# Layer-norm sums with 128 output columns, idle products on TensorE, twelve partial means ahead of the last convolution, and a weight split behind the transposes

## The chip, the cores and the metric

The kernel runs on one core of a Trainium2 chip. The metric is the device time of one launch in microseconds. TensorE multiplies (and its clock has two levels here, 1.2 and 2.4 GHz), VectorE, ScalarE and GpSimd work element by element, SyncE issues DMAs. The engines run their own instruction streams and meet at semaphores.

## What is computed

One step of a streaming encoder with two layers, for 1024 prompt frames and 8 streams of 16 frames (1152 columns in all), model width 1024, float32. The change lies in the convolution module of layer 0 and in the last norm:

```python
def conv_module(h, buf, w_pw1, b_pw1, w_dw, b_dw, ln_g, ln_b, w_pw2, b_pw2):
    u = h @ w_pw1 + b_pw1
    a, gt = jnp.split(u, 2, axis=-1)
    glu = a * jax.nn.sigmoid(gt)
    xp = jnp.concatenate([buf.astype(glu.dtype), glu], axis=1)
    new_buf = xp[:, xp.shape[1] - (CONV_K - 1):]
    y = causal_dwconv(xp, w_dw, b_dw)          # 31 taps for each channel
    y = jax.nn.silu(layernorm(y, ln_g, ln_b))
    return y @ w_pw2 + b_pw2, new_buf

def rmsnorm(x, g):                             # also the last step of all
    y = x * lax.rsqrt(jnp.mean(x * x, axis=-1, keepdims=True) + EPS)
    return y * g
```

Behind it stand a ConvFFN, an HGRN2 mixer with its own ConvFFN, and the final RMSNorm.

## The kernel before

Activations lie by features: X holds 8 channel blocks (KD) of 128 partitions by 1152 columns, worked in three thirds of 384 (`third(c)`, NCH = 3). A float32 product is made of three products of high and low parts (XH, XL, WH, WL), 384 columns each, into one of two sets of three PSUM banks (`ps_bank(n, c)`; n is the number of the tile, its parity the set). MB are the two remaining banks. Weights come in 196 units of 128x1024, loaded by SP into two slots, split by GpSimd into high and low parts (`split(u)`: a cast and a subtraction), and used by TensorE in `big`.

First pointwise convolution: tiles G and V of each channel block go to VectorE, which forms the GLU. The depthwise convolution of blocks 0, 2 and 4 is done tap by tap on VectorE; that of the blocks 1, 3, 5, 6, 7 (TOEPLITZ) on TensorE: VectorE transposes the GLU in 32x32 pieces (`forward`, which raises `xt_rdy`), eight DMAs bring the taps as small Toeplitz matrices (`blocks`), TensorE makes 32 groups of two products with 40 columns (`convolved`), ScalarE copies the banks out (`by_blocks`) and VectorE transposes back (`back`). A float32 product of this kind leaves two MATMUL records in the profile; a high or low part leaves one. For blocks 1, 3, 5 and 6 the convolution is woven into the products of the next V tile. Block 7 has no such tile behind it. There TensorE weaves in the layer norm's mean: `mean(k, c)` multiplies channel block k of third c with a matrix of -1/1024, accumulated over k; 21 of these (blocks 0 to 6) are the list `parts`. Seven of them stand ahead of the convolution of block 7 and 14 between its two-group steps (16 steps); three for block 7 (L745, waiting for `back(7)`) stand behind it.

Then the layer norm, by thirds. `centred` (VectorE, L1763, 8 instructions a third) adds bias and mean, `ln_squares` (ScalarE) squares, GpSimd adds squares in pairs (L593), and `variance(c)` (L822) sums over channels: for each of four pairs and three pieces of 128 tokens, the squares are the stationary side and a column of ones the moving side, so that one output column holds 128 sums. ScalarE takes the root (`ln_root`), VectorE the reciprocal, spread on a diagonal (`diagonal`, L1770 and L1772), TensorE multiplies the diagonal with ones (`spread_norm`, L834), VectorE scales (`ln_scaled`, L1782), ScalarE applies gain, bias and SiLU (L1349) and casts every second block (L1352; GpSimd the others), VectorE forms the low part (`ln_low`, L1790), and TensorE begins the second pointwise convolution (`ln_row`, L857).

The order on each engine is the order of the program text: no planner, only waits on semaphores. GpSimd's splits of units U_PW2 and U_PW2 + 1 (the first two of the second pointwise convolution) follow the splits of the first one at once; behind them stand the pair sums and the casts of the norm. SP loads a unit when the split of the unit two before it is done.

The final norm has the same shape: `fin_sum` (L1164), the root, `fin_diagonal`, `fin_over` (L1179, spread), `scaled_out` on VectorE (L2205) and GpSimd's share, and the output DMAs.

Of the kernel before, what the change touches and what calls it, by code (L numbers as in the profile page):

```python
# [6 lines left out]
ACT = mybir.ActivationFunctionType  # L7
# [5 lines left out]
P = 128  # L13
D = 1024
# [3 lines left out]
KD = D // P  # L18
# [4 lines left out]
TOEPLITZ = (1, 3, 5, 6, 7)  # L23
BLK = 32
# [8 lines left out]
NCH = 3  # L33
COLS = SEQ // BLK + NB
BANK_GROUPS = 12
CW = T // NCH
# [27 lines left out]
T_PW2 = T_PW1 + len(PW1)  # L64
# [31 lines left out]
T_MEAN, T_VAR = pw1_tile("MEAN", 0), pw1_tile("VAR", 0)  # L96
# [78 lines left out]
def build(nc, d_w, d_x, d_par, d_taps, d_ffp, d_fhist, d_chist, d_state, d_const, d_mask,  # L175
          o_y, o_convp, o_convs, o_hgp, o_hgs, o_ffn):
    with ExitStack() as ctx:
# [15 lines left out]
        CONST = sb("CONST", [P, 2 * P + NB])  # L193
        IDENT = CONST[:, 0:P]
        ONES = CONST[:, P:2 * P]
# [3 lines left out]
        EPSC = SMALL[:, 0:1]  # L199
        LB = SMALL[:, 1:1 + KD]  # L200
        OMLB = SMALL[:, 1 + KD:1 + 2 * KD]
        R9 = SMALL[:, 1 + 2 * KD:1 + 2 * KD + TCH]
# [45 lines left out]
        LSQ = cut(NCH * KD, CW, of=HGA)  # L248
# [45 lines left out]
        PS, MB = BANKS[:, 0:2 * NCH, :], BANKS[:, 2 * NCH:8, :]  # L294
# [6 lines left out]
        def ps_bank(n, c):  # L301
            return PS[:, (n % 2) * NCH + c, 0:CW]
# [42 lines left out]
        xt_rdy, bt_rdy, bt_free, str_rdy = sem("xt_rdy"), sem("bt_rdy"), sem("bt_free"), sem("str_rdy")  # L345
# [175 lines left out]
        def _(pool):  # L521
            def split(u, i=0, per=0, used=None):


                s = u % 2
                pool.wait_ge(raw_ld[s], lin(i, 8 * per, raw_count(u)))
                if U_HG <= u - 2 < U_WO:
                    pool.wait_ge(a_full, u - 2 - U_HG + 1)
                elif used is None and u >= 2:
                    used = (unit_tile(u - 2) + 1, 0)  # L530
                if used is not None:
                    pool.wait_ge(ps_full, lin(i, used[1], used[0]))

                one = WRAW[:, s, 0:1]
                nc.gpsimd.tensor_tensor(PAD, one, one, ALU.mult)  # L535
                nc.gpsimd.tensor_copy(WH[:, s, :], WRAW[:, s, :]).then_inc(w_hi, 1)  # L536
                pool.wait_ge(w_hi, lin(i, per, u + 1))
                nc.gpsimd.tensor_tensor(WL[:, s, :], WRAW[:, s, :], WH[:, s, :].bitcast(F32),  # L538
                                        ALU.subtract).then_inc(w_split, 1)
# [44 lines left out]
            nc.gpsimd.memset(WT_FLAT[:, half:], 0.0).then_inc(wt_zero, 1)  # L584
            for u in range(3, U_PW2):
                split(u)
            split(U_PW2)
            split(U_PW2 + 1)

# [42 lines left out]
        def _(pe):  # L632
            def free_slot(n, i=0, per=0):

                if per or n >= 2:
                    pe.wait_ge(ps_free[n % 2], lin(i, per // 2, n // 2))
# [101 lines left out]
            def mean(k, c):  # L738

                if c == 0 and k in TOEPLITZ:  # L740
                    pe.wait_ge(bt_free, TOEPLITZ.index(k) + 1)
                    pe.wait_ge(str_rdy, TOEPLITZ.index(k) + 1)
                elif c == 0:
                    pe.wait_ge(taps_done, len([c for c in range(k + 1) if c not in TOEPLITZ]))
                ins = nc.tensor.matmul(ps_bank(T_MEAN, c), NEG_MEAN, X[:, k, third(c)], start=False, stop=k == KD - 1,  # L745
                                       skip_group_check=True)
                if k == KD - 1:
                    ins.then_inc(mean_full, 1)
# [43 lines left out]
            for c in range(1, KD):  # L792
                if c > 1:
                    big(pw1_tile("G", c), U_PW1 + 2 * c)
                big(pw1_tile("V", c), U_PW1 + 2 * c + 1, between=with_conv(c - 1) if c - 1 in TOEPLITZ else None)

            free_slot(T_MEAN)
            pe.wait_ge(mg_rdy, 1)
            for c in range(NCH):
# [1 line left out]
                                 skip_group_check=True)  # L801

            parts = [(k, c) for k in range(KD - 1) for c in range(NCH)]
            ahead = len(parts) - (BLK // 2 - 2)
            for k, c in parts[:ahead]:
                mean(k, c)
            for g in range(0, BLK, 2):
                convolved(KD - 1, g, g + 2)
                if g // 2 < len(parts) - ahead:
                    mean(*parts[ahead + g // 2])  # L810
            for c in range(NCH):
                mean(KD - 1, c)

            def variance(c):

                if c == 0:
                    free_slot(T_VAR)
                for p in range(KD // 2):
                    pe.wait_ge(pair_rdy, KD // 2 * c + p + 1)
                    for t in range(NCH):  # L820

                        ins = nc.tensor.matmul(ps_bank(T_VAR, c)[:, t:t + 1],  # L822
                                               LSQ[:, KD * c + 2 * p, t * P:(t + 1) * P], ONES[:, 0:1],
                                               start=p == 0 and t == 0, stop=p == KD // 2 - 1 and t == NCH - 1,
                                               skip_group_check=True)
                ins.then_inc(var_full, 1)

            def spread_norm(c):

                pe.wait_ge(yd_rdy, c + 1)  # L830
                if c == 2:
                    pe.wait_ge(yn_rdy, KD)
                for t in range(NCH):
                    ins = nc.tensor.matmul(MB[:, c % 2, t * P:(t + 1) * P], ONES,  # L834
                                           DIAG[:, c * CW + t * P:c * CW + (t + 1) * P], start=True, stop=True)
                ins.then_inc(spread_full, 1)

            variance(0)
            variance(1)
            spread_norm(0)  # L840
            variance(2)
            spread_norm(1)
            spread_norm(2)

            pe.wait_ge(w_split, U_PW2 + 2)
            free_slot(T_PW2)
            free_slot(T_PW2 + 1)

            def ln_row(j, c, k):
# [14 lines left out]
            for j in range(2):  # L866
                for k in range(KD):
                    ins = ln_row(j, NCH - 1, k)
# [284 lines left out]
            def fin_sum(c):  # L1153

                if c == 0:
                    pe.wait_ge(mb_free, M_FIN)
                pe.wait_ge(acc_rdy, c + 1)
                for squares in (ACC, SQ[:, 1, :]):
                    if squares is not ACC:
                        pe.wait_ge(last_sq, c + 1)  # L1160
                    for t in range(NCH):
                        a = c * CW + t * P

                        ins = nc.tensor.matmul(MB[:, c % 2, t:t + 1], squares[:, a:a + P], ONES[:, 0:1],  # L1164
                                               start=squares is ACC and t == 0,
                                               stop=squares is not ACC and t == NCH - 1, skip_group_check=True)
                ins.then_inc(fin_sums, 1)
# [27 lines left out]
        def _(act):  # L1195
# [135 lines left out]
            def ln_root(c):  # L1331

                act.wait_ge(var_full, c + 1)
                A(R9[:, c * NCH:(c + 1) * NCH], ps_bank(T_VAR, c)[:, 0:NCH], ACT.Sqrt, bias=EPSC, scale=1.0 / D
                  ).then_inc(root_rdy, 1)

            ln_squares(0)
# [212 lines left out]
                A(SQ[:, 1, third(c)], X[:, KD - 1, third(c)], ACT.Square).then_inc(last_sq, 1)  # L1550
            for c in range(NCH):
                act.wait_ge(fin_sums, c + 1)
                A(R9[:, c * NCH:(c + 1) * NCH], MB[:, c % 2, 0:NCH], ACT.Sqrt, bias=EPSC, scale=1.0 / D
                  ).then_inc(fin_root, 1)
            for c in range(NCH):
                act.wait_ge(fin_twice, c + 1)
# [768 lines left out]
```

## Time and profile before

| | us |
|---|---|
| median of 3 runs | 2890.31 (2889.29 to 2891.17) |
| profiled execution | 2888.88 |
| its span, first to last instruction | 2887.10 |
| TensorE busy | 2849.4 (99%) |
| VectorE busy | 1662.5 (58%) |
| GpSimd busy | 834.4 (29%) |
| ScalarE busy | 529.3 (18%) |
| mean granted TensorE clock | 0.986 |

All times in the views are microseconds from the start of the span. A granted clock of 1.00 is 2.4 GHz, 0.50 is 1.2 GHz. PE is TensorE's products, PEld its weight loads, DVE VectorE, ACT ScalarE, POOL GpSimd; a name with q is the engine's queue that issues DMAs. A record names the line of the kernel, the operation, output <- inputs and shapes.

### The profile page before, as it was taken

Reading aid. Unit: us, or ns where it says so; the run is one execution under the profiler, and the core shown is the slowest. Engines: PE = TensorE matmul, PEld = TensorE weight load, DVE = VectorE, ACT = ScalarE, POOL = GpSimd, SP = SyncE. Lnnn points to the kernel's source line nnn. Section 1 sums busy time; section 2 is a strip of 40 time slices with the busy share of each in tenths; the row PEclk is TensorE's granted clock in tenths of the full one; section 3 lists DMA queues with packets and bytes.
Section 4 is the critical chain, followed back from the end, with each engine's and each line's share of the span. In section 5 each row is a group of like instructions: output and inputs, shape, how many; then the busy total and the mean of one; then the engine's idle time right before and its main releaser. Section 6 shows DMA issues by size and latency. Waiting matters only on the chain.

```text
span 2887.1 us, 40334 instructions
## 1 busy us (share of the span) xinstructions
PE 2849.4 (99%) x16832; PEld 2798.9 (97%) x16832; DVE 1662.5 (58%) x1821; ACT 529.3 (18%) x647; POOL 834.4 (29%) x686
## 2 busy tenths in 40 slices
PE   8999999999999999999999999999999999999998
PEld 8999799999999999999999999989999999999998
DVE  8995336454545455466676667781744555454445
ACT  3001323111111111231111111121311111111122
POOL 5221154222222222243121222114322222222224
PEclk9999599999999999999999999999999999999999
DMA  5223021111111111121111110103111111111112
GB/s 152 57 59 57 0 109 44 38 43 44 44 38 41 44 44 40 41 108 52 46 45 38 45 46 31 47 30 116 38 43 44 44 39 41 44 44 39 41 45 79
DMA packets 109012, 147.07 MB, mean 51 GB/s; under 512 B 65265, under 2 KB 78065, under 8 KB 108913
## 3 DMA queue, kind: packets, MB, share of 16 engines
q1 hardware_dynamic: 48624, 112.48, 12.3%
q10 hardware_dynamic: 60288, 33.14, 4.0%
q8 instruction: 78, 1.28, 0.2%
q14 instruction: 22, 0.17, 0.0%
HBM read 129.13 MB, written 16.47 MB: 50 GB/s over the span
## 4 chain that ended last, share of the span: by engine, by line
PE 89%; DVE 9%; issue 1%; ACT 1%; POOL 0%; DMA 0%; DVEq 0%; ACTq 0%; POOLq 0%
PE BANKS L649 63%; PE BANKS L895 11%; PE BANKS L937 3%; PE BANKS L1123 3%; DVE BANKS L1678 1%; PE BANKS L722 1%; PE BANKS L720 1%; PE BANKS L857 1%; DVE HGA L2032 1%; DVE HGA L1997 1%; DVE HGA L2019 1%; PE BANKS L745 1%; DVE XL L1590 1%; PE BANKS L986 1%; DVE X L1678 1%
## 5 line engine op out<-in xcount | busy, mean ns | idle before, releaser
L535 POOL TENSOR_TENSOR SMALL<-WRAW 128x1 f32<-128x1 f32 x196 | 48.4, 247 | 1916.3 <-PE BANKS L649 1334.1
L649 PE MATMUL BANKS<-XH,WH 128*128 128x384 f32 x2592 | 592.0, 336 | 0.6 <-DVE X L1603 0.5
L649 PE MATMUL BANKS<-XL,WH 128*128 128x384 f32 x2592 | 588.6, 334 | 0.0
L649 PE MATMUL BANKS<-XH,WL 128*128 128x384 f32 x2592 | 588.6, 334 | 0.0
L538 POOL TENSOR_TENSOR WL<-WRAW,WH 128x1024 fp32r<-128x1024 f32 x196 | 476.5, 2431 | 15.7
L649 PEld LDWEIGHTS BANKS<-XL,WH 128*128 128x128 f32 x2592 | 462.2, 188 | 0.0
L649 PEld LDWEIGHTS BANKS<-XH,WL 128*128 128x128 f32 x2592 | 462.1, 188 | 0.0
L649 PEld LDWEIGHTS BANKS<-XH,WH 128*128 128x128 f32 x2592 | 460.4, 188 | 1.7 <-DVE X L1603 0.9
L1815 DVE TENSOR_TENSOR X<-BANKS,X 128x1152 f32<-128x1152 f32 x168 | 228.0, 1357 | 267.4 <-PE BANKS L649 206.4
L1872 DVE SCALAR_TENSOR_TENSOR ARENA<-ARENA 128x1168 f32<-128x1168 f32 x176 | 255.7, 1453 | 130.9 <-ACT ARENA L1377 122.2
L1377 ACT ACTIVATE ARENA<-ARENA 128x1168 f32<-128x1168 f32 x88 | 120.3, 1367 | 943.7 <-DVE ARENA L1612 943.7
L649 PE MATMUL BANKS<-GH,WH 128*128 128x384 f32 x1050 | 242.1, 338 | 3.1 <-DVE X L1817 1.6
L649 PE MATMUL BANKS<-GL,WH 128*128 128x384 f32 x1050 | 241.4, 338 | 0.0
L649 PE MATMUL BANKS<-GH,WL 128*128 128x384 f32 x1050 | 241.4, 338 | 0.0
L1863 DVE COPY ARENA<-ARENA 128x2 f32 (+1 forms) x88 | 15.1, 172 | 382.7 <-PE BANKS L649 382.4
L536 POOL CAST WH<-WRAW 128x1024 fp32r<-128x1024 f32 x196 | 204.9, 1045 | 0.2
L649 PEld LDWEIGHTS BANKS<-GH,WH 128*128 128x128 f32 x1050 | 188.5, 188 | 5.1 <-DVE X L1815 2.8
L649 PEld LDWEIGHTS BANKS<-GH,WL 128*128 128x128 f32 x1050 | 189.0, 188 | 0.0
L649 PEld LDWEIGHTS BANKS<-GL,WH 128*128 128x128 f32 x1050 | 188.8, 188 | 0.0
L895 PE MATMUL BANKS<-XH,WH 128*128 128x384 f32 x744 | 182.6, 353 | 2.6 <-DVE HGA L1970 2.3
L895 PE MATMUL BANKS<-XL,WH 128*128 128x384 f32 x744 | 169.6, 335 | 0.0
L895 PE MATMUL BANKS<-XH,WL 128*128 128x384 f32 x744 | 169.3, 335 | 0.0
(214 smaller groups left out, 3474.7 us busy)
## 6 DMA issues: line engine op xcount, KB each, us to landing
WRAW<-in_w SPq DMA_DIRECT2D x188, 512.0 KB, 3.5
X<-in_x SPq DMA_DIRECT2D x8, 576.0 KB, 9.0
X<-in_x ACTq DMA_DIRECT2D x8, 576.0 KB, 7.2
x_kept<-X ACTq DMA_DIRECT2D x8, 576.0 KB, 2.8
X<-x_kept ACTq DMA_DIRECT2D x8, 576.0 KB, 7.4
HGA<-taps_padded ACTq DMA_DIRECT2D x32, 128.0 KB, 3.5
HGA<-in_state ACTq DMA_DIRECT2D x8, 512.0 KB, 4.3
out_hgs<-HGA ACTq DMA_DIRECT2D x8, 512.0 KB, 2.6
```

What stands on the lines that cost most here:

```text
L535: nc.gpsimd.tensor_tensor(PAD, one, one, ALU.mult)
L536: nc.gpsimd.tensor_copy(WH[:, s, :], WRAW[:, s, :]).then_inc(w_hi, 1)
L538: nc.gpsimd.tensor_tensor(WL[:, s, :], WRAW[:, s, :], WH[:, s, :].bitcast(F32), ALU.subtract).then_inc(w_split, 1)
L649: ins = nc.tensor.matmul(ps_bank(n, c), w, x[:, third(c)], start=(k == 0 and q == 0), stop=(k == last and q == 2), skip_group_check=betwee ...
L720: nc.tensor.matmul(out, WT[:, g, 0, :], XT[0][:, :, g], start=True, stop=False, skip_group_check=True)
L895: ins = nc.tensor.matmul(big_place(what, h)[:, c, :], w, x[:, k, third(c)], start=(k == 0 and q == 0), stop=(k == KD - 1 and q == 2), skip ...
L937: ins = nc.tensor.matmul(chunk(what, c), KRS[h % 2][:, a], QFS[h % 2][:, a], start=True, stop=True)
L1123: ins = nc.tensor.matmul(ps_bank(T_HG + m, c), w, x[:, k, third(c)], start=(k == 0 and q == 0), stop=(k == KD - 1 and q == 2), skip_group_ ...
L1377: A(C[:, half, 0:CE], U[:, half, 2:EXT], ACT.Identity, bias=CB[:, at], scale=FFP[:, at, FW2:FW2 + 1].rearrange("p a b -> p (a b)")).then_i ...
L1678: dc.inc(V.scalar_tensor_tensor(out=dst, in0=src, scalar=w, in1=sums, op0=ALU.mult, op1=ALU.add))
L1815: ins = V.tensor_tensor(pieces(X[:, m, :]), ps(n), pieces(X[:, m, :]), ALU.add)
L1872: return V.scalar_tensor_tensor(out=c, in0=u[:, k:k + CE], scalar=FFP[:, at, k:k + 1] .rearrange("p a b -> p (a b)"), in1=c, op0=ALU.mult, ...
```

## The change

Five edits.

1. In GpSimd's stream a wait is put ahead of `split(U_PW2)`: for `xt_rdy` at 5, the transposes of block 7.
2. `ahead`, the number of partial means ahead of the last convolution, becomes 12 where it was 21 - 14 = 7. Nine are left for its steps; each of the other seven steps gets an idle product: float32, 256 columns, the identity as the stationary side and constants as the moving side, into the first MB bank, which nobody reads.
3. Six idle products behind the convolution, two behind the means of block 7; in the norm two ahead of `spread_norm(1)`, one ahead of and three behind `spread_norm(2)` (into bank 2 of tile T_PW2, whose `free_slot` wait moves up with them).
4. `variance` and `fin_sum` multiply with 128 columns of ones instead of one, so that each sum stands 128 times in a row of the bank.
5. ScalarE's roots read every 128th column.

```diff
@@ GpSimd
             for u in range(3, U_PW2):
                 split(u)
+
+            pool.wait_ge(xt_rdy, len(TOEPLITZ))
             split(U_PW2)
             split(U_PW2 + 1)
@@ TensorE
+            def idle_products(times, out):
+
+                for _ in range(times):
+                    nc.tensor.matmul(out[:, 0:2 * P], IDENT, CONST[:, 0:2 * P], start=True, stop=True)
+
@@
-            ahead = len(parts) - (BLK // 2 - 2)
+            ahead = 12
             for k, c in parts[:ahead]:
                 mean(k, c)
             for g in range(0, BLK, 2):
                 convolved(KD - 1, g, g + 2)
                 if g // 2 < len(parts) - ahead:
                     mean(*parts[ahead + g // 2])
+                else:
+                    idle_products(1, MB[:, 0, :])
+
+            idle_products(6, MB[:, 0, :])
             for c in range(NCH):
                 mean(KD - 1, c)
+            idle_products(2, MB[:, 0, :])
@@ variance
-                        ins = nc.tensor.matmul(ps_bank(T_VAR, c)[:, t:t + 1],
-                                               LSQ[:, KD * c + 2 * p, t * P:(t + 1) * P], ONES[:, 0:1],
+
+                        ins = nc.tensor.matmul(ps_bank(T_VAR, c)[:, t * P:(t + 1) * P],
+                                               LSQ[:, KD * c + 2 * p, t * P:(t + 1) * P], ONES,
@@
             variance(2)
+            free_slot(T_PW2)
+            idle_products(2, ps_bank(T_PW2, 2))
             spread_norm(1)
+            idle_products(1, ps_bank(T_PW2, 2))
             spread_norm(2)
+            idle_products(3, ps_bank(T_PW2, 2))
             pe.wait_ge(w_split, U_PW2 + 2)
-            free_slot(T_PW2)
             free_slot(T_PW2 + 1)
@@ fin_sum
-                        ins = nc.tensor.matmul(MB[:, c % 2, t:t + 1], squares[:, a:a + P], ONES[:, 0:1],
+                        ins = nc.tensor.matmul(MB[:, c % 2, t * P:(t + 1) * P], squares[:, a:a + P], ONES,
@@ ScalarE, the two roots
-                A(R9[:, c * NCH:(c + 1) * NCH], ps_bank(T_VAR, c)[:, 0:NCH], ACT.Sqrt, bias=EPSC, scale=1.0 / D
+                A(R9[:, c * NCH:(c + 1) * NCH], ps_bank(T_VAR, c)[:, 0:CW:P], ACT.Sqrt, bias=EPSC, scale=1.0 / D
@@
-                A(R9[:, c * NCH:(c + 1) * NCH], MB[:, c % 2, 0:NCH], ACT.Sqrt, bias=EPSC, scale=1.0 / D
+                A(R9[:, c * NCH:(c + 1) * NCH], MB[:, c % 2, 0:CW:P], ACT.Sqrt, bias=EPSC, scale=1.0 / D
```

## Rows read from the trace of the kernel before

**Rows 1.** The page: TensorE's granted clock in 40 slices, and the chain by engine.

```profile
PEclk9999599999999999999999999999999999999999
PE 89%; DVE 9%; issue 1%; ACT 1%; POOL 0%; DMA 0%; DVEq 0%; ACTq 0%; POOLq 0%
```

**Rows 2.** Busy time by windows: window, length, PE, PEld, DVE, ACT, POOL, PEclk, DMA, GB/s.

```profile
246.60:249.70 3.10, 2.97 (x26) 2.84 (x26) 2.81 (x3) 0.46 (x2) 2.71 (x3) 1.00 0.18 17
...
253.20:272.30 19.10, 19.10 (x147) 19.10 (x148) 0.00 (x0) 0.00 (x0) 0.00 (x0) 1.00 0.01 5
...
287.40:328.20 40.80, 40.80 (x140) 32.80 (x139) 0.66 (x4) 1.98 (x2) 0.00 (x0) 0.50 0.00 0
...
335.10:338.40 3.30, 2.55 (x19) 2.33 (x19) 3.30 (x7) 3.29 (x7) 3.12 (x4) 1.00 0.02 5
338.60:352.10 13.50, 11.94 (x57) 11.85 (x57) 11.69 (x25) 7.76 (x17) 7.87 (x8) 0.50 0.00 0
...
355.60:382.00 26.40, 25.51 (x147) 25.24 (x147) 20.53 (x40) 20.96 (x36) 12.08 (x16) 1.00 0.24 92
...
2871.20:2877.90 6.70, 6.70 (x33) 6.70 (x33) 6.32 (x14) 1.25 (x3) 3.17 (x4) 0.50 0.70 252
```

**Rows 3.** The chain that ended last, 283 to 345 us: start, us, what.

```profile
283.81 1.16 issue
...
286.05 0.71 PE BANKS L745 x2
286.75 0.16 PE BANKS L720 x2
286.92 0.22 PE BANKS L722 x2
...
290.69 1.43 PE BANKS L745 x2
...
293.68 1.43 PE BANKS L745 x2
...
328.27 0.71 ACT HGA L1275
...
330.63 1.66 PE BANKS L745 x2
...
332.32 12.69 DVE X L1763 x24
```

**Rows 4.** Timeline, 241 to 282 us: start, us, engine, line, operation, operands, count.

```profile
241.81 1.29 DVE L1656 SCALAR_TENSOR_TENSOR HGA<-HGA,PAR,X 128x1024 f32<-128x1024 f32 x1
...
276.98 2.35 POOL L538 TENSOR_TENSOR WL<-WRAW,WH 128x1024 fp32r<-128x1024 f32 x1
...
277.22 3.19 DVE L1656 SCALAR_TENSOR_TENSOR HGA<-HGA,PAR,X 128x1024 f32<-128x1024 f32 x1
277.37 4.68 PE L745 MATMUL BANKS<-X,NEG_MEAN 128*128 128x384 f32 x14
```

**Rows 5.** The chain that ended last, 346 to 382 us.

```profile
346.28 1.65 PE BANKS L834 x6
347.93 4.92 PE BANKS L822 x24
...
356.54 25.40 PE BANKS L857 x144
```

**Rows 6.** Timeline of the two norms.

```profile
334.10 8.35 POOL L593 TENSOR_TENSOR HGA<-HGA 128x384 f32<-128x384 f32 x8 [54.77 <-ACT HGA L1329]
335.24 0.80 PE L822 MATMUL BANKS<-CONST,HGA 128*128 128x1 f32 x6 [0.40 <-POOL HGA L593]
...
350.51 1.95 DVE L1782 TENSOR_TENSOR X<-BANKS,X 128x384 f32<-128x384 f32 x4
353.38 0.56 DVE L1772 TENSOR_TENSOR ARENA<-CONST,SMALL 128x384 f32<-128x384 f32 x1
...
2869.60 0.74 PEld L1179 LDWEIGHTS BANKS<-ARENA,CONST 128*128 128x128 f32 x6
...
2875.00 6.39 DVE L2205 SCALAR_TENSOR_TENSOR X<-X,PAR,BANKS 128x384 f32<-128x384 f32 x12 [0.34 <-PE BANKS L1179]
```

## The prediction

> **What bounds the kernel now.** I read the page first: TensorE carries 89% of the chain that ended last, and in the forty slices its granted clock falls well below full in one slice only, the fifth, 289 to 361 us [rows 1]. The windows of that stretch [rows 2] give the levels: 1.00 (2.4 GHz) from 253.2 to 272.3, 0.50 (1.2 GHz) from 287.4 to 328.2, back to 1.00 at 335.1, 0.50 from 338.6 to 352.1, 1.00 from 355.6. So the path runs through TensorE at half clock in the last depthwise convolution, and after it through VectorE's centring (12.69 us) with TensorE at half clock behind it [rows 3, 5]. From 356.54 the chain is TensorE's products one behind another [rows 5], nearly to the end. What the change moves up to 356.54 is therefore carried to the end almost whole.
>
> What TensorE did before each turn [rows 2, 3, 4]: it had no product from 282.05 to 284.98, then took 40-column convolution products and single means; the mean at 286.05 still took 0.71 us, the later ones 1.43, and the clock stayed down for 40.8 us in the same mix. At 246.6 to 249.7 it ran convolution products and little else, and the clock fell too, and came back after 384-column products. From 253.2 to 272.3, with eight convolution products between each nine wide ones, it held. It came back by 335.1 after three means in a row, and by 355.6 after variance and spread products in a run.
>
> **Part 1: twelve partial means ahead of the convolution instead of seven.** Seven means (14 records) take 4.68 us, 0.668 each [rows 4]. Twelve end at 277.37 + 12 x 0.668 = 285.39. Before, TensorE stood idle till 284.98: the transposes were done at 283.81 and "issue" fills the rest [rows 3]; the tap DMAs, for which the first convolution product waits as well, are the likely last releaser. So the start moves by +0.41 us, the idle 2.93 us goes, and five means leave the convolution. The five use channel blocks 2 and 3, which VectorE's order finishes ahead of block 5's GLU, long before; blocks 4 to 6 are now wanted no sooner than at the first steps of the convolution, as before, and block 6, put back at the very last, only in the seventh. Cost of the start: 0.4 us; gain: what follows.
>
> **Part 2: idle products inside the convolution.** A step of the loop is four convolution products and a mean: 0.16 + 3 x 0.22 + 0.71 = 1.53 us at full clock, and at half clock 2.99 from one mean (290.69) to the next (293.68), of which 1.43 is the mean's and 1.56 the convolution's [rows 3]. An idle product has 256 columns; between the 384-column mean (0.668) and the 128-column spread product (six records' loads in 0.74 us, so some 0.24 a product) [rows 4, 6] it takes two thirds of a mean, 0.45, plus the 0.04 that a mean pays between convolutions: 0.49. With the clock full: 9 x 1.53 + 7 x (0.82 + 0.49) = 22.9 us, the last convolution product 0.49 before that, at 285.39 + 22.45 = 307.8. Before it ended at 328.25 [rows 3]. **-20.4 us.** No edit adds a wait on TensorE here. Nearly the whole forecast hangs on the clock in this one term; all others are about a microsecond.
>
> **Part 3: idle products while the last block is put back.** From the last convolution product to the first mean of block 7 there were 2.38 us (328.25 to 330.63), set by ScalarE's copy and VectorE's transposes [rows 3], whose pace doesn't hang on TensorE's clock. Seven idle products (one from the loop, six behind it) take 7 x 0.45 = 3.2 us. They outlast the wait: **+0.8 us**. The mean itself took 1.69 us till VectorE could start [rows 3]; at full clock 0.67 and some 0.3 of latency: **-0.7 us**. The centring then starts near 312.0 instead of 332.32: -20.3 us together.
>
> **Part 4: the normalisation.** VectorE's 24 centrings stay 12.69 us. Variance products with 128 columns instead of one: six one-column records took 0.80 us at full clock, weight loads included, and six 128-column records of the spread products have their six loads in 0.74 us [rows 6]. Loading the weights sets the pace of either, so I price the columns at nothing; the ends are -0.1 and +0.1 us for the last one's own length. The Trainium skill has a table that speaks against that: "TensorE: Matmul & The Clock Gate" (Back-to-back issue gap) gives about 25 ns from one narrow matmul to the next and about 56 ns at 128 columns, for matmuls by themselves. By it the 24 records behind the first spread would cost 24 x 31 ns = 0.7 us more, as an estimate; this trace's one-column records, each with a weight load, stand 0.12 us apart, so the table does not bear on them.
>
> From the end of the centring the old chain is: diagonal, spread 0 (1.65), variance 2 (4.92), root, table load, SiLU, split, first product at 356.54 [rows 5]. At full clock spread 0 and variance 2 take 0.75 + 24 x 0.114 = 3.5 us instead of 6.57, 3.1 less. But what is late next: VectorE's first scalings end at 352.46, it then needs 0.8 us for diagonal 2 and 0.56 for the next scaling, 0.56 for the low part [rows 5, 6]: 354.4 on the old scale. And TensorE stands behind its own padding: spread 2 waits for diagonal 2 (353.3 on that scale), takes 0.8, then three idle products take 1.4: 355.5. So at full clock the first product comes 1.1 us earlier than 356.54, not 3.1.
>
> Will the clock be full there? Between the end of variance 1 and spread 0 nothing fills TensorE: block pairs come every 1.04 us from GpSimd (8.35 for eight) [rows 6], the eighth at 342.45, its products end at 343.2, and spread 0 waits till 346.28: 3.0 us without a product, as long as the idle time before 284.98, which preceded a fall. I expect one fall in that gap, and the return during variance 2 and the idle products behind it. Then variance 2 ends near 352.4 on the old scale, and two idle products, spread 1, one idle product, spread 2 and three idle products, at full clock 0.9 + 0.8 + 0.45 + 0.8 + 1.4, lead to 356.7: the gain is eaten, **0 us**. Ends: -1.1 (full clock), and +4.3 with half clock throughout: 352.85 + 1.8 + 1.4 + 0.9 + 1.3 + 2.6 = 360.8.
>
> **Part 5: weight split behind the transposes.** In the trace GpSimd's 2.35 us subtraction at 276.98 lies on VectorE's 1024-element multiply, which took 3.19 us where the same one at 241.81 took 1.29 [rows 4]. The wait lets both splits start after the fifth transpose pair: XT is ready 1.9 us sooner, near 281.9. Queued behind the waiting GpSimd are the two splits (3.5 us each, done near 289), then pair sums wanted near 314; SP's next two weight loads, which wait for these splits, go out near 285 and 289 and are wanted by splits behind the casts of the normalisation, after 330. Covered by 25 us and more; without that cover 7 us. The loads also leave the tap DMAs alone. But TensorE is busy with its means till 285.39, so all this is worth 0 (ends 0 and 0).
>
> **Part 6: the final norm.** 128 columns again: price nothing, at most +0.1 on the first two sums. After 2871.2 the clock was 0.50 [rows 2] while only thin sums had been run; with wide ones it may hold. VectorE then lost 0.34 us waiting for the second spread [rows 6], and the rest is VectorE's and the output DMAs' pace: **-0.2 us** (ends -0.4, +0.2).
>
> **The sum.** +0.4 - 20.8 (together -20.4), +0.8, -0.7, 0, 0, -0.2 = -20.5 us. Against the profiled execution (2888.88 us, its span 2887.10 and 1.78 around it) that gives 2868.4; its median run is 2890.31, 1.4 higher, so the forecast of the median is 2890.3 - 20.5 = **2869.8 us**.
>
> **Rivals.** *A, full clock in the normalisation too:* for it, TensorE is denser at the start of that stretch than before; against it, the unfilled 3.0 us. -1.1: 2868.7. It differs by less than the runs do. *B, the clock falls inside the convolution when the means run out:* a step then has 256 idle columns in place of 384, closer to the stretch 246.6 to 249.7 that fell. Seven steps at 1.56 + 0.93 instead of 1.31 (+8.3), padding behind them partly at half (+2.5), mean at half (+0.7), normalisation +1: -8, 2882. *C, slower:* the filled gap doesn't hold the clock, which falls near the start of the convolution as before and can't return in that mix. Nine steps of 2.99 and seven of 1.56 + 0.93, less the last idle product, end the convolution at 328.8, +0.6; then 7 x 0.9 = 6.3 us of idle products stand where 2.38 were waited, +3.9; half clock in the normalisation +4.3: +8.8, 2899. It decides if the clock is 0.50 for most of the convolution: with the +8.2 behind it, ten of its sixteen steps at half clock (1.46 us more each with a mean, 1.18 without) use up the rest of the gain. Against it: 253.2 to 272.3 held for 19 us, and a mean per four convolution products is no thinner. *D, the change does nothing,* since products of the identity and constants don't count for the clock: then the nine mean steps must hold it alone, and the padding fails: near B. Against it, the spread products have a nearly empty diagonal and the clock came back on them [rows 2].
>
> **Chances.** Forecast 0.50, A 0.32, B and D 0.10, C 0.06, something unnamed but small 0.02. Range: 2867 to 2880, which leaves out C, most of B and little below; it takes in the ends of the unknown costs (-2, +5 around 2870). A measurement of this kernel tells 0.2%, 5.8 us, from no change. Faster 0.92, same 0.02, slower 0.06.
>
> **What would show it.** The windows of the profile after: clock 1.00 through the convolution, its last product near 308 (right), or 0.50 from anywhere inside (B, C). No idle time before it, and XT near 282. First mean of block 7 behind idle products and not behind VectorE's transpose, near 311. Centring from 312. One stretch of 0.50 after some 323 (forecast) or none (A). Variance records 0.11 us apart at full clock. First product of the second pointwise convolution near 336. All wrong if the clock doesn't follow TensorE's density but something that this trace doesn't show.

## The result and the profile after

The changed kernel takes 2865.26 us (median of 4 executions, 2864.53 to 2865.57), the kernel before in the same job 2890.74: ratio 0.9912 (95% interval 0.9895 to 0.9930), 25.5 us less. Forecast: 20.5 less, 2869.8, range 2867 to 2880. The direction is right, the clock in the last convolution did what was forecast, and the time lies 1.7 us below the range. The profiled execution took 2864.53 us, its span 2862.7.

The page first: the fifth slice, which stood at 5 [rows 1], reads 9 (90% or more) like the others.

```profile
PEclk9999999999999999999999999999999999999999
```

The windows of the profile after (columns as in [rows 2]): the woven convolution of block 6, the end of the means, the last convolution, the wait and means behind it, the norm, and the end:

```profile
248.60:272.80 24.20, 24.07 (x177) 23.96 (x176) 0.19 (x1) 3.78 (x4) 0.00 (x0) 1.00 0.04 5
280.50:283.00 2.50, 2.50 (x11) 1.53 (x9) 0.88 (x1) 1.49 (x3) 2.42 (x2) 1.00 0.39 57
283.00:305.50 22.50, 22.50 (x159) 19.81 (x158) 3.63 (x4) 2.08 (x3) 3.76 (x4) 1.00 0.18 47
305.50:309.30 3.80, 3.80 (x18) 3.17 (x18) 1.57 (x2) 1.04 (x2) 0.00 (x0) 1.00 0.01 4
309.40:320.30 10.90, 9.35 (x56) 7.09 (x54) 10.90 (x21) 10.16 (x20) 8.02 (x8) 1.00 0.00 0
320.40:323.30 2.90, 0.07 (x1) 0.00 (x0) 2.81 (x6) 2.90 (x8) 2.42 (x3) 1.00 0.00 0
323.80:327.10 3.30, 3.30 (x17) 3.30 (x17) 2.41 (x6) 0.00 (x0) 1.26 (x2) 0.50 0.00 0
327.20:332.40 5.20, 5.20 (x37) 4.80 (x37) 4.00 (x10) 3.67 (x6) 0.23 (x1) 1.00 0.00 0
```

The convolution, 40.8 us at 0.50 before [rows 2], is 22.5 us at 1.00. TensorE doesn't wait ahead of it, and in this part of the profile the only stretch at 0.50 is the one behind the unfilled wait for the first spread (320.4 to 323.3: PE 0.07 us of 2.90). The chain of the profile after, in the same stretch as [rows 3, 5]:

```profile
275.23 7.74 PE BANKS L747 x24
282.96 0.16 PE BANKS L722 x2
...
283.80 0.71 PE BANKS L747 x2
...
297.64 0.49 PE BANKS L802 x2
...
305.59 3.08 PE BANKS L802 x14
308.68 0.66 PE BANKS L747 x2
309.33 0.03 issue
309.36 12.69 DVE X L1779 x24
...
323.30 1.31 PE BANKS L847 x6
324.61 3.93 PE BANKS L835 x24
328.55 0.86 PE BANKS L802 x4
```

L802 is the idle product, L747 the mean, L835 the variance, L847 the spread. The mean keeps its 0.71 us from the first to the last step where it had gone to 1.43, and the idle product inside the loop takes the 0.49 that was forecast.

Both profiles cut at the same places, in us (the ends of records in the timelines of both):

| stretch | before | after | difference | forecast |
|---|---|---|---|---|
| start to first partial mean | 277.37 | 275.06 | -2.31 | 0 |
| first partial mean to last convolution product | 50.87 | 30.53 | -20.34 | -20.4 |
| to the first mean of block 7 | 2.39 | 2.92 | +0.53 | +0.8 |
| to the start of the centring | 1.69 | 0.85 | -0.84 | -0.7 |
| to the second pointwise convolution | 24.22 | 22.89 | -1.33 | 0 |
| to the end of the span | 2530.55 | 2530.49 | -0.06 | -0.2 |

The main term came to 0.1 us of its forecast. Two rows didn't come out: the norm, and 2.31 us ahead of anything that the change touches on TensorE.

### The profile page after: what moved, and what is told of

Read it like the earlier page. It is cut to its first block, busy times and chain, and to the rows that moved or that the text cites. A ratio compares the mean times of both kernels' runs of the same rounds, so it can differ in the third digit from the quotient of the medians.

```text
span 2862.7 us, 40417 instructions
## 1 busy us (share of the span) xinstructions
PE 2826.8 (99%) x16874; PEld 2780.2 (97%) x16874; DVE 1662.8 (58%) x1821; ACT 529.3 (18%) x647; POOL 834.9 (29%) x686
## 4 chain that ended last, share of the span: by engine, by line
PE 91%; DVE 7%; issue 1%; ACT 0%; POOL 0%; DMA 0%; DVEq 0%; ACTq 0%; POOLq 0%
PE BANKS L651 64%; PE BANKS L911 11%; PE BANKS L953 3%; PE BANKS L1139 3%; PE BANKS L724 1%; PE BANKS L873 1%; PE BANKS L722 1%; DVE HGA L2048 1%; DVE BANKS L1694 1%; DVE HGA L2013 1%; DVE HGA L2035 1%; DVE XL L1606 1%; PE BANKS L1002 1%; PE BANKS L747 1%; PE BANKS L992 1%
```

## The experiments

**Twelve partial means alone.**

```diff
-            ahead = len(parts) - (BLK // 2 - 2)
+            ahead = 12
```

> The kernel before with one line changed: twelve partial means ahead of the last convolution instead of seven; no idle products, sums with one column, split where it was. Theory (the clock follows how densely TensorE works; the filled 2.93 us gap is what matters first): the clock is 1.00 through the nine steps with a mean and falls only in the seven bare steps; the convolution takes 9 x 1.53 + 7 x 0.87 to 1.70 = 20 to 26 us instead of 43.3, the norm stays as before; 15 to 21 us faster than before, 2870 to 2876. Rival (without idle products the convolution can't hold the clock): 0.50 within some 4 us of its start, gain 5 x 1.43 - 0.4 - 0 us at most 4 us: 2886 to 2889.

Measured: 2869.12 us (2866.43 to 2870.46) against 2890.72, ratio 0.9917 (0.9899 to 0.9935). One line brings 21.6 of the 25.5 us. Its windows: the nine steps with a mean and some bare ones, the last bare steps, the centring, the norm:

```profile
285.50:303.40 17.90, 17.90 (x129) 15.52 (x128) 0.85 (x5) 3.48 (x4) 0.00 (x0) 1.00 0.06 9
303.60:307.30 3.70, 3.70 (x18) 3.56 (x17) 0.00 (x0) 0.00 (x0) 0.00 (x0) 0.50 0.00 0
307.40:313.60 6.20, 3.90 (x6) 1.85 (x6) 3.78 (x7) 2.43 (x5) 0.44 (x1) 0.50 0.00 0
...
317.20:341.00 23.80, 21.32 (x89) 20.97 (x90) 19.76 (x42) 17.04 (x33) 10.46 (x13) 0.50 0.00 1
```

In the convolution the clock fell only when 40-column products stood by themselves; behind it, it came back for some 3 us and was at half again through the norm. The rival, 2886 to 2889, is out; the time is 1 us under the theory's 2870 to 2876.

**The wait filled with idle products, nothing moved.**

```diff
+            for _ in range(7):
+                nc.tensor.matmul(MB[:, 0, 0:2 * P], IDENT, CONST[:, 0:2 * P], start=True, stop=True)
             for g in range(0, BLK, 2):
```

> The kernel before with seven idle products (3.1 us) put between the seven partial means and the last convolution, and nothing else changed. Theory (what the wait of 2.93 us did to the clock is the cause; it doesn't matter what fills it): the convolution runs at 1.00 through its fourteen steps with a mean, 14 x 1.53 + 2 x 0.87 to 1.7 = 23 to 25 us instead of 43.3; 17 to 21 us faster than before, 2870 to 2874. Rival (products of an identity with constants don't count, only real work moved into the wait does): 0.50 from about 287 as before, 2890 to 2891.

Measured: 2868.67 us (ten executions; nine from 2866.56 to 2872.60, one at 2888.68). The time of nine is at or under the theory's 2870 to 2874, as with real work in the wait. In the profiled one the windows read:

```profile
279.90:283.00 3.10, 3.03 (x15) 2.31 (x13) 2.89 (x5) 0.31 (x1) 0.00 (x0) 1.00 0.74 158
283.20:306.00 22.80, 22.80 (x153) 19.09 (x153) 0.97 (x5) 3.50 (x4) 0.00 (x0) 1.00 0.05 7
```

So products of an identity with constants kept the clock in this place as the means did. The one at 2888.68 has a mean clock of 0.987, as executions of the kernel before have; it has no trace, so where its clock fell is not shown.

**Seven means ahead, all else changed.**

```diff
-            ahead = 12
+            ahead = 7
```

> The changed kernel with seven partial means ahead of the convolution again, so that the wait for the tap matrices and transposes is open; all else stays (fourteen means and two idle products in the steps). Theory (the open wait is what puts the clock down, and the mix of the steps can't bring it back): 0.50 from about 2 us into the convolution through fourteen steps of 2.99, then the eight idle products in a row bring it back: the convolution ends 17 to 20 us later than in the changed kernel, 2882 to 2887. Rival (128 columns and idle products hold the clock in any case): 1.00 throughout, within 1 us of the changed kernel.

Measured: 2865.20 us in the median of five: four from 2863.57 to 2865.41 and one, the profiled, at 2886.04. Neither side had it: the theory had named a fall, the rival none, and by the times there were both. TensorE's row at the head of the convolution shows that the wait was no longer the old one:

```profile
281.06 0.40 PE L722 MATMUL BANKS<-HGA 128*128 128x40 f32 x2 [1.30 <-issue]
```

1.30 us of idle time and not 2.93. With the split behind the transposes, VectorE's multiply takes 1.28 us where it had taken 3.19 [rows 4]; what the last part of the wait is for ("issue"), the tap matrices most likely, is not shown. So the split's place, which the forecast priced at 0, had to be tried by itself.

**The split alone.**

```diff
+            pool.wait_ge(xt_rdy, len(TOEPLITZ))
             split(U_PW2)
```

> The kernel before with GpSimd's wait ahead of the split and nothing else: seven means ahead, one-column sums, no idle products. Theory (the length of the wait ahead of the convolution decides, and the split makes it: VectorE's multiply takes 1.3 us again and the weight load leaves the tap DMAs alone): the wait is 1.3 to 1.5 us instead of 2.93; in most executions the clock then holds through the steps with a mean, 2866 to 2871, and in some it falls, 2885 to 2890. Rival, the prediction's own step (the split is worth nothing on the path; the convolution's clock needs the filled wait): 2887 to 2890 in every execution.

Measured: 2869.44 us in the median of ten: seven from 2864.39 to 2871.30 and three from 2887.57 to 2891.05; ratio 0.9956 (0.9927 to 0.9985) over all. The wait in its profile is 0.95 us (1.3 to 1.5 had been expected) and the convolution holds:

```profile
284.70:285.60 0.90, 0.01 (x1) 0.04 (x1) 0.89 (x2) 0.31 (x1) 0.90 (x2) 1.00 0.39 60
285.70:309.00 23.30, 23.30 (x156) 19.55 (x156) 4.21 (x5) 3.50 (x4) 5.88 (x5) 1.00 0.21 52
```

Most executions held and some did not, as the theory had it. The edit that the forecast priced at nothing brings some 20 us in seven of ten executions when it stands alone. This profile had also lost some 4.8 us ahead of the convolution: the clock was at half from 249.7 to 259.8, and the first mean starts at 279.97.

**Padding and columns with the wait open.** The changed kernel with seven means ahead and without GpSimd's wait.

```diff
-            pool.wait_ge(xt_rdy, len(TOEPLITZ))
-            ahead = 12
+            ahead = 7
```

> The changed kernel with seven means ahead and without GpSimd's wait: the wait ahead of the convolution is open and, with the split where it was, some 2.9 us long; padding and 128 columns stay. It is the run with seven ahead and padding (there the wait was 1.3 us, and one execution of five fell) with a longer wait. Theory (length of the wait): the clock falls in nearly every execution, 2883 to 2888. Rival (padding or columns made the falls rare there, not the short wait): one execution in five or fewer, the others 2864 to 2867.

Measured: 2888.51 us (2886.80 to 2903.67), ratio 1.0007 (0.9989 to 1.0025): all ten executions at the old level or above. The profile, at the wait, behind it, and in the steps:

```profile
279.90:282.10 2.20, 0.00 (x0) 0.00 (x0) 1.99 (x4) 0.00 (x0) 0.00 (x0) 1.00 0.94 190
282.20:284.10 1.90, 1.90 (x14) 1.64 (x14) 1.15 (x2) 0.84 (x2) 0.00 (x0) 1.00 0.41 61
284.30:326.50 42.20, 42.20 (x146) 34.13 (x146) 0.71 (x4) 2.73 (x4) 0.00 (x0) 0.50 0.00 0
```

With this wait, 2.37 us and not the 2.9 expected, the clock falls each time, whatever idle products and wide columns stand behind it. Against the run with seven means ahead and all else changed, only the place of the split differs. Side by side, for the clock in the last convolution:

| wait ahead of it | kernel | held |
|---|---|---|
| 2.9 us | before | 3 of 51 |
| 2.4 us | seven means, split first, padded | 0 of 10 |
| 1.3 us | seven means, split moved, padded | 4 of 5 |
| 0.9 us | before with the split moved | 7 of 10 |
| filled with idle products | before + 7 | 9 of 10 |
| none, twelve means | changed | 4 of 4 |

"Held" is read from the time, some 20 us apart, and agrees with the clock wherever there is a profile; the length of the wait is that of the one profiled execution. It is a chance, and the place of the split moves it (0 of 10 against 4 of 5, 3 of 51 against 7 of 10). That it does so by the length of the wait is argued: the run with the filled wait shows that a wait without products is what counts, but no run varies the length alone, and 1.3 and 0.9 us are not told apart by so few. Twelve means ahead held in all 22 executions of five more kernels below and above (alone, split first, no padding, padding moved, means spread). With one column beside them an execution took 2885.70 us at a mean clock of 0.990, just what the fallen one of the padded seven shows; it has no trace, so a fall with twelve means ahead is not excluded. The three of the kernel before that held took 2865.79, 2866.11 and 2867.09 us; its two profiled executions, which are not among the 51, fell.

**Twelve means, split first.**

```diff
-            pool.wait_ge(xt_rdy, len(TOEPLITZ))
```

> The changed kernel without GpSimd's wait ahead of the first split of the second pointwise convolution. Theory (the split is covered, worth 0; what the changed kernel gained ahead of the convolution, 2.3 us in its profile, is chance of that execution): VectorE's multiply of block 7 takes 3.2 us instead of 1.3, the transposes end some 1.9 us later, TensorE starts the convolution behind its twelve means as before: same time within 0.7 us, 2865. Rival (the 2.3 us came from the moved split, which no longer meets VectorE near 247): 1.5 to 2.3 us slower, 2867 to 2867.6, with the clock falling near 249.

Measured: 2865.73 us (2864.45 to 2867.84). VectorE's multiply takes 3.19 us again, and TensorE's first convolution product waits:

```profile
283.24 0.40 PE L721 MATMUL BANKS<-HGA 128*128 128x40 f32 x2 [0.31 <-issue]
```

From the first mean to the centring it is 34.84 us for the changed kernel's 34.30. So the split is worth some 0.5 us on top of the twelve means, not quite nothing, and the means hide the rest of it. Its first mean stands at 275.03, as in the changed kernel, though the split is at its old place: the 2.3 us don't come from the split.

**The kernel before, a second profile.**

> The kernel before, unchanged, for a second profile. Theory (the 2.3 us by which the changed kernel was ahead before it reached the change are chance: a fall at 249.7 and VectorE's order against GpSimd near 79 us): the first mean starts anywhere between 275.0 and 277.5 us or, with more falls in the woven convolutions, later; the clock falls in the last convolution whatever came before. Rival (it belongs to the kernel): the first mean at 277.4 within 0.2 us, with a fall near 249.

Measured: 2886.37 us; bias and first mean at 273.19 and 275.13, no fall at 249; the last convolution at 0.50 as ever:

```profile
246.60:249.70 3.10, 2.97 (x24) 2.84 (x24) 2.28 (x2) 1.04 (x2) 3.02 (x2) 1.00 0.40 44
...
285.30:326.00 40.70, 40.70 (x140) 32.67 (x139) 0.52 (x4) 1.97 (x2) 0.00 (x0) 0.50 0.00 0
```

The 2.31 us ahead of the change don't belong to every execution of the kernel: this one reaches the first mean 2.24 us sooner than the first one. Of all fourteen profiles ten have it between 275.03 and 275.23; the others are the kernel before (277.37), twelve means alone (277.42), the split alone (279.97) and bare steps (286.86). Against this second profile the changed kernel's span is 21.9 us shorter, not 24.4.

**One column again.**

```diff
-        ps_bank(T_VAR, c)[:, t * P:(t + 1) * P], ..., ONES,
+        ps_bank(T_VAR, c)[:, t:t + 1], ..., ONES[:, 0:1],       # and so in fin_sum and in both roots
```

> The changed kernel with the sums of both norms multiplied by one column again (and read so). Theory (columns are work that keeps the clock, their own time is nothing): the convolution is unchanged at 1.00; in the norm the clock falls when the one-column sums run, about 3 to 5 us after they begin, and the padding behind is at half clock; the first product of the second pointwise convolution comes 1 to 4 us later than in the changed kernel; in the final norm 0.3 us later: 2866.5 to 2870. Rival (128 columns bring nothing, or cost their own time): equal or up to 0.7 us faster, 2864.5 to 2865.5.

Measured: 2869.61 us in the median of eight (five from 2868.38 to 2870.06, and 2873.45, 2877.65, 2885.70), ratio 0.9932 (0.9907 to 0.9956). In its profile centring to second pointwise convolution takes 25.74 us, 2.85 more than in the changed kernel, and the final norm to the end 21.26 against 20.00. The clock, and what is beside it:

```profile
309.40:315.70 6.30, 4.89 (x30) 3.75 (x28) 6.30 (x13) 5.61 (x11) 4.38 (x5) 1.00 0.00 0
315.90:332.80 16.90, 15.22 (x67) 14.69 (x67) 12.49 (x26) 10.24 (x21) 7.60 (x8) 0.50 0.00 0
```

PE is busy 90% of the second window and the clock is down; most of its records are one column wide. A busy share doesn't tell whether the clock holds. But the 4 us are not the columns' share of the 25. The one-column norm without padding took 24.21 or 24.22 us in five profiles (the kernel before twice, twelve means, filled wait, split alone), so here the padding at half clock makes it longer, and with 128 columns it takes 22.8 with or without padding: the columns bring some 1.4 us. In the final norm the same five took 19.99 to 20.32 us with one column, and eight profiles with 128 columns 19.85 to 20.00: there the columns bring some 0.2 us, and most of the 1.26 that this profile lost is its own. The three late executions have no trace, and where they lose is open.

**Bare steps.**

```diff
                     mean(*parts[ahead + g // 2])
-                else:
-                    idle_products(1, MB[:, 0, :])
```

> The changed kernel without the seven idle products between the last convolution steps; the six behind it stay. Theory (40-column products by themselves don't hold the clock, as at 246.6 to 249.7 in the kernel before): the clock falls to 0.50 during the bare steps or just behind them; steps of 0.87 us become 1.7, the idle products behind take 0.9 each: 0 to +5 us against the changed kernel, 2865 to 2870. Rival (the idle products in the loop are not needed): the clock stays 1.00 and their 7 x 0.49 us less one are saved: -3 us, 2862.

Measured: 2865.94 us, but from 2862.03 to 2877.48. The profiled one is the 2877.48, and 11.8 us of its loss lie ahead of the first mean: the clock fell in the woven convolution of block 1 and stayed down for 20 us; in the last convolution it fell in the bare steps.

```profile
81.80:102.10 20.30, 18.29 (x73) 18.29 (x73) 20.30 (x27) 1.25 (x1) 0.54 (x1) 0.50 0.08 27
...
309.00:313.80 4.80, 4.80 (x45) 4.80 (x45) 0.00 (x0) 0.99 (x1) 0.00 (x0) 1.00 0.00 0
314.00:320.60 6.60, 6.60 (x21) 5.52 (x21) 1.57 (x2) 1.01 (x2) 0.00 (x0) 0.50 0.00 0
```

First convolution product to centring: 26.75 us, in the changed kernel 26.42. Both readings occur: the profile shows the theory's fall, and 2862.03 is the rival's time. In the median the seven idle products bring nothing that can be told from zero.

**No padding behind the convolution and in the norm.**

```diff
-            idle_products(6, MB[:, 0, :])        # and the 2, 2, 1 and 3 behind it
```

> The changed kernel without the idle products behind the convolution and in the norm (14 of them); the seven in the loop, the twelve means ahead and the 128 columns stay. Theory (padding there is a wash): the first mean of block 7 comes 2.4 us behind the convolution instead of 2.9; the clock falls in the wait before the first spread as in the changed kernel, and comes back on variance and spread products; the start of the second pointwise convolution moves by -1 to +1.5 us: 2864 to 2867. Rival (the padding carries the clock through the norm): 0.50 from the wait for block 7 on, variance products at half clock, 2 to 4 us slower, 2867.5 to 2869.5.

Measured: 2863.84 us (2862.97 to 2864.84), 1.4 us less than the changed kernel. Last convolution product to first mean 2.41 us (2.92 with padding), centring to second pointwise convolution 22.78 (22.89). The clock did what neither side had said. It fell in the wait for block 7 too, where TensorE stood idle for 1.92 us, and was down through the first variance products:

```profile
308.90:315.70 6.80, 6.16 (x22) 4.58 (x22) 6.77 (x13) 6.02 (x12) 4.80 (x5) 0.51 0.01 2
```

It cost nothing, since VectorE's centring is the path there. The padding costs a little and brings nothing; the time is just under the theory's 2864, the rival's 2867.5 is out.

**Padding moved to the open wait.**

```diff
-            idle_products(6, MB[:, 0, :])
+            idle_products(4, MB[:, 0, :])
             variance(1)
+            idle_products(5, MB[:, 1, :])
             spread_norm(0)
             ...                                   # 3, 1 and 1 for 2, 1 and 3 around the other spreads
```

> The changed kernel with the padding moved: four instead of six idle products behind the convolution, five new ones in the unfilled wait before the first spread, three instead of two ahead of the second spread, one instead of three behind the last. Theory (the padding outlasts two waits and leaves out the one that matters): clock 1.00 from the convolution to the final norm; centring 0.8 us sooner behind the convolution, the second pointwise convolution 22.2 us behind the centring's start instead of 22.9: 1 to 1.6 us faster than the changed kernel, 2863.7 to 2864.3. Rival (the waits are set by VectorE and ScalarE, so no padding matters): within 0.5 us of it.

Measured: 2863.17 us (2862.31 to 2864.02), 2.1 less than the changed kernel. The wait ahead of the first spread and all up to the final norm:

```profile
320.00:323.00 3.00, 2.31 (x13) 1.70 (x11) 2.88 (x6) 3.00 (x9) 2.47 (x3) 1.00 0.00 0
323.00:330.20 7.20, 7.03 (x52) 6.39 (x52) 6.18 (x15) 3.51 (x7) 1.73 (x2) 1.00 0.00 0
330.30:2852.20 2521.90, 2509.25 (x14892) 2475.49 (x14890) 1392.42 (x1476) 462.15 (x563) 741.88 (x581) 1.00 0.15 48
```

Centring to second pointwise convolution is 21.27 us, 0.9 less than the 22.2 of the theory. Against no padding at all the median is 0.7 us lower, and the executions of the two overlap. And variance 2 at full clock with 128 columns:

```profile
323.74 2.51 PE L835 MATMUL BANKS<-CONST,HGA 128*128 128x128 f32 x21
```

**Means spread over all sixteen steps, no idle products in the loop.** On top of the last one:

```diff
-                if g // 2 < len(parts) - ahead:
-                    mean(*parts[ahead + g // 2])
-                else:
-                    idle_products(1, MB[:, 0, :])
+                rest = len(parts) - ahead
+                done, due = g // 2 * rest // (BLK // 2), (g // 2 + 1) * rest // (BLK // 2)
+                if due > done:
+                    mean(*parts[ahead + done])
```

> The kernel with the moved padding (four idle products behind the convolution, five ahead of the first spread, three ahead of the second, one behind the last), and the seven idle products in the loop taken out, the nine means spread evenly over the sixteen steps instead of standing in the first nine. Theory (density over a few steps is what counts, and nine means in sixteen steps are enough): clock 1.00 through the convolution, which takes 7 x 0.49 - 0.49 = 2.9 us less; 2860.3 from 2863.2. Rival (a step pair with one mean is too thin): the clock falls within the convolution in some executions and can't return: 2868 to 2885 in those.

Measured: 2859.07 us (2858.78 to 2860.58 in five, 2863.83 in one) against 2889.56, ratio 0.9905 (0.9879 to 0.9932). This is the fastest version: 6.2 us less than the changed kernel (median against median of two jobs), 1.2 below the theory. The convolution:

```profile
283.00:302.30 19.30, 19.30 (x145) 17.18 (x144) 3.62 (x4) 2.08 (x3) 3.74 (x4) 1.00 0.24 55
302.40:317.00 14.60, 13.05 (x70) 9.67 (x70) 12.84 (x24) 11.52 (x22) 8.02 (x8) 1.00 0.01 1
```

19.41 us from first to last product instead of 22.65, all of it wanted work, and the clock holds.

## Why the prediction was right, and where it was wrong

The mechanism of the main term held. What failed is the size of two parts of the sum, the norm (part 4) and the base, and they are worked out below.

**The clock in the last convolution: right.** The twelve means and the convolution at full clock take 30.53 us from first mean to last product, for 8.0 + 22.45 = 30.5 forecast, and the idle product takes its 0.49 us (small errors cancel: 7.9 us for 8.0 in the means, 22.65 for 22.45 behind them). In the profiled executions with twelve means the clock never fell while steps held a mean or an idle product, so rivals B, C and D didn't happen there. The twelve means alone bring nearly all of it; the seven idle products in the loop, to which part 2 owed the clock of its last steps, bring nothing that can be told from zero, and without them and with the means spread the kernel is faster.

**Part 5, the split, priced at 0: nearly right beside the twelve means (0.5 us), wrong as to what it does.** The prediction saw VectorE 1.9 us sooner and stopped at "TensorE is busy with its means till 285.39". It did not ask what a shorter wait does by itself to the clock. Two edits cover each other: the means remove all of the wait and the split most of it, and alone one brings 21.6 us and the other some 20 us in most executions. The forecast needed neither number, so the time did not suffer from it.

**Part 3, padding and first mean: right in sign and size**, +0.53 and -0.84.

**Part 4, the norm: the term was mis-sized, -1.33 us measured for 0 forecast.** The fall in the unfilled wait came as forecast, but lasted 3.4 us, from 323.71 to 327.12, and ended within variance 2: this took 3.93 us, not close to its old 4.92, and ended 19.2 us behind the start of the centring where 20.1 were forecast. From there on it was 3.7 us for the forecast 4.3. The step that failed is the price of the columns: they were priced by their own time alone, and what they do to the clock was put at nothing. Without any padding the stretch is 22.78 us, with one column and no padding 24.2, so the 1.4 us are the columns' doing. Their own time was judged right: 2.51 us for 21 records at full clock in the kernel with the padding moved is 0.12 each, and six one-column records took 0.80 us [rows 6] (the sum took 0.114 each, 0.1 us less for the 24). The Trainium skill's table in "TensorE: Matmul & The Clock Gate" (Back-to-back issue gap), for matmuls by themselves, would put 128 columns some 31 ns above one; these products, each with a weight load, don't show it.

**Part 6, the final norm: right in size.** It was 20.18 to 20.00 us from the first sum to the end in this pair of profiles, for the -0.2 forecast; the second profile of the kernel before took 19.99, but over five profiles with one column and eight with 128 some 0.2 us remains.

**The base: wrong, and it put the time outside.** The sum started from one profiled execution and moved the result by 1.4 us to the median, as if the changed kernel's executions would lie as they did before. In that profiled execution time had been lost ahead of the change, in a wait of 0.5 us near 81 and a fall at 249.7 to 253.2, that the second profile of the same kernel hasn't:

```profile
81.30 0.79 PE L649 MATMUL BANKS<-XH,WH 128*128 128x384 f32 x3 [0.50 <-DVE X L1603]
249.80:253.10 3.30, 3.30 (x13) 3.30 (x12) 0.00 (x0) 1.01 (x1) 0.73 (x1) 0.50 0.60 147
```

Of the 4.5 us between 2869.8 and 2865.26, 1.5 are in the stretches that the change touches (-22.04 from the first mean on, for -20.5, nearly all of it the norm's), 2.3 stand ahead of them, and 0.7 come from the step to the median: the changed kernel's lies 0.73 us above its profiled execution, not 1.43. The range allowed 2.8 us below the value. The 1.5 us alone would have stayed inside, the 3.0 us that no term of the sum held would not.

Whether those 3.0 us are chance stays open. The medians of the kernel before were 2890.7, 2890.7, 2889.1 and 2889.6 us in four jobs, and its executions lay between 2865.8 and 2910.2, so a profile can easily stand 2 us off. But three of the five profiles of kernels made from the one before were late at the first mean, and one of the nine made from the changed one. All four executions of the kernel before that stand beside the result lie 2.9 us or more above its second profile (2886.37 us), and the changed kernel's four lie within 1.04 us. Why the medians differ by 25.5 us where the two undisturbed profiles differ by 21.9 is not shown.

## What to carry to other kernels

Where the granted clock of a stretch is half, look at the wait that stands ahead of it, and shorten it or fill it with work that has to be done anyway; inside, try spreading the dense products evenly before adding idle ones. Two edits that close the same wait are worth one, and padding is worth looking for only where a wait is really open. When a clock can fall by chance, one profile is not a base: compare stretches between marks, and take the base from several executions. And what it costs to take an edit out of the finished kernel (4 us for the columns) is not what the edit had brought (some 1.6 us).

## What the runs showed of the hardware

The fall is a matter of chance with the same program: three of 51 executions of the kernel before held the clock through the last convolution and 48 did not. In the profiled execution with bare steps it fell in a convolution woven with wide products and stayed at 1.2 GHz for 20 us, though that mix had held for 19.1 us at 2.4 GHz elsewhere [rows 2].

The same mix can keep either level once it is there: the steps of the last convolution with four convolution products and a mean ran 40.8 us at 1.2 GHz in the kernel before and 22.8 us at 2.4 GHz behind the filled wait.

A PE that the profile calls busy 90% of a stretch of 16.9 us stayed at 1.2 GHz when most of its records were one column wide. With 128 columns, which take the same 0.12 us a record at full clock, it was back at 2.4 GHz after 3.4 us, within variance 2 of the changed kernel.

Products with the identity as weights and an identity and ones as the moving side held the clock as well as data, in nine of ten executions with the filled wait.
